# Two RMS norms inside a two-layer decoder trunk: the first weight block behind each multiplies the unnormalised x, and the division by the rms follows when the product is read out of PSUM

## What is computed

```python
def rms_norm(x, g):
    y = x * lax.rsqrt(jnp.mean(x * x, axis=-1, keepdims=True) + NORM_EPS)
    return y * g

def even_layer(h, ...):
    proj = rms_norm(h, norm_mix) @ w_in
    ...                                    # S5 state space model and block attention
    h = h + concatenate([y_a, y_b]) @ w_out
    return h + swiglu(rms_norm(h, norm_ffn), w_gate, w_up, w_down)      # norm 1, FFN of 2816

def odd_layer(h, ...):
    proj = rms_norm(h, norm_mix) @ w_in                                 # norm 2, 2756 columns
    ...                                    # RWKV-7 time mixing and sparse attention
    h = h + concatenate([y_c, y_d]) @ w_out
    return h + moe_swiglu(rms_norm(h, norm_ffn), router, e_gate, e_up, e_down)   # 8 experts, top 2
```

## Time and profile before

| | us |
|---|---|
| median of 3 runs | 1647.14 |
| lowest and highest of them | 1647.04, 1648.26 |
| the profiled execution, device time | 1645.62 |
| its span in the trace | 1643.8 |
| PE busy | 1550.2 (94% of the span) |
| DVE busy | 439.0 (27%) |
| ACT busy | 294.0 (18%) |

### The profile page before, as it was taken

How to read it: one execution, slowest core, us unless ns; L and a number is a source line. 1 busy time by engine, 2 the same in 40 slices (tenths; PEclk the granted TensorE clock), 3 DMA queues, 4 the chain that set the end, 5 groups by cost and what they waited for, 6 DMA issues and landing times.

```text
span 1643.8 us, 47174 instructions
## 1 busy us (share of the span) xinstructions
PE 1550.2 (94%) x22217; PEld 1464.2 (89%) x22217; DVE 439.0 (27%) x857; ACT 294.0 (18%) x515; POOL 19.3 (1%) x21
## 2 busy tenths in 40 slices
PE   7898999999946899999999999999999999999997
PEld 6667999998934788899999999999999999999996
DVE  6843354546387632100100100100100000100102
ACT  3233344334234211100000100100001001001002
POOL 0000000000001210000000000000000000000000
PEclk9999999999966998899999999999999999999998
DMA  9121555363300035599999999999999999999980
GB/s 316 58 99 53 205 204 181 128 230 105 147 0 1 3 111 212 189 385 356 377 373 359 374 383 348 372 382 357 369 380 360 369 384 355 363 384 357 370 318 28
DMA packets 135648, 425.22 MB, mean 259 GB/s; under 512 B 9786, under 2 KB 12964, under 8 KB 135332
## 3 DMA queue, kind: packets, MB, share of 16 engines
q1 hardware_dynamic: 133536, 420.59, 68.1%
q10 hardware_dynamic: 1924, 1.64, 0.4%
HBM read 421.18 MB, written 1.05 MB: 257 GB/s over the span
## 4 chain that ended last, share of the span: by engine, by line
PE 87%; DVE 9%; ACT 2%; issue 1%; DMA 0%; ACTq 0%; SPq 0%; DVEq 0%
PE bank L2242 34%; PE bank L2240 20%; PE bank L1885 5%; PE bank L1887 5%; PE bank L1886 5%; PE bank L2220 2%; PE bank L1860 2%; PE bank L2261 1%; PE bank L1629 1%; PE bank L1873 1%; PE bank L1795 1%; PE bank L1878 1%; PE bank L2228 1%; PE bank L1619 1%; DVE xnT L966 1%
## 5 line engine op out<-in xcount | busy, mean ns | idle before, releaser
L2242 PE MATMUL bank<-ring,yT 128*32 128x128 f32 x8064 | 889.1, 273 | 0.0
L2240 PE MATMUL bank<-ring,yT 128*32 128x384 f32 x8064 | 877.7, 487 | 1.0 <-ACT yT L886 1.0
L2242 PEld LDWEIGHTS bank<-ring,yT 128*32 128x32 f32 x8064 | 876.5, 110 | 0.0
L2240 PEld LDWEIGHTS bank<-ring,yT 128*32 128x32 f32 x8064 | 299.8, 109 | 11.7 <-issue 10.5
L1560 DVE TENSOR_TENSOR arena<-arena,bank 128x384 f32<-128x384 f32 x56 | 28.9, 551 | 635.2 <-PE bank L2242 635.2
L1887 PE MATMUL bank<-arena_r,ring_r 128*128 128x256 f32 x688 | 193.4, 281 | 0.0
L1885 PE MATMUL bank<-yT_r,ring_r 128*128 128x256 f32 x512 | 144.8, 283 | 5.2 <-DVE arena_r L1199 5.2
L1886 PE MATMUL bank<-yT_r,ring_r 128*128 128x256 f32 x512 | 144.5, 282 | 0.0
L1887 PEld LDWEIGHTS bank<-arena_r,ring_r 128*128 128x128 f32 x688 | 131.0, 190 | 0.0
L1194 DVE TENSOR_TENSOR ring_r<-ring,ring_r 128x2048 fp32r<-128x2048 f32 (+1 forms) x46 | 99.0, 2153 | 114.5 <-ACT ring_r L706 114.4
L902 ACT ACTIVATE yT<-bank 128x384 f32<-128x384 f32 x56 | 25.0, 491 | 560.5 <-PE bank L2261 560.5
(11 more groups left out here) (435 smaller groups left out, 1278.9 us busy)
## 6 DMA issues: line engine op xcount, KB each, us to landing
ring<-in_moe_w_gate SPq DMA_DIRECT2D x56, 2048.0 KB, 9.4
ring<-in_moe_w_up SPq DMA_DIRECT2D x56, 2048.0 KB, 9.4
ring<-in_moe_w_down SPq DMA_DIRECT2D x56, 2048.0 KB, 9.8
ring<-in_ffn_w_gate SPq DMA_DIRECT2D x5, 2048.0 KB, 7.8
ring<-in_ffn_w_up SPq DMA_DIRECT2D x5, 2048.0 KB, 7.8
ring<-in_ffn_w_down SPq DMA_DIRECT2D x5, 2048.0 KB, 8.9
ring<-in_o_w_in SPq DMA_DIRECT2D x5, 2048.0 KB, 7.8
ring<-in_e_w_in SPq DMA_DIRECT2D x4, 2048.0 KB, 16.8
```

Source lines behind the costliest of these rows:

```text
L2240: pe_.matmul(b[QUAD[m], 0:FM], x(m), w[:, 0:FM], start=start, stop=stop, skip_group_check=True)
L2242: last = pe_.matmul(b[QUAD[3], P * m:P * m + P], x(m), w[:, FM:FB], start=start and m == 0, stop=stop, skip_group_check=True)
```

## The change

At norm 1 and norm 2 the first block (gate 0, block 25) no longer waits for the rms. ACT writes `hT * g` rounded into the high part (`scaled_hi`, a copy with a scale per partition, eight instructions of 128 x 256), DVE writes `hT * g` minus that into the low part (`scaled_lo`, eight instructions of 128 x 256), both between the adds into `hT`. PE multiplies the first block with these. The products for the square sums stand inside its first half: four behind strip 1, two behind strip 2, two behind strip 3. The square root, the reciprocal and `xnT` come as before, and `split_xn` writes the normed high and low parts over the unnormalised ones, each half once PE has multiplied it; the second block (up 0, block 26) is the first to use them. The first block's result is multiplied by `rstd` by DVE (`by_rstd`, two instructions of 128 x 512): at norm 1 from PSUM into `gate_s`, where ACT then takes silu in place; at norm 2 from PSUM into `raw`, in place of `odd_copy(0)` and `odd_copy(1)` on ACT. The `keep_warm` products of both norms are gone, in front and behind. At norm 1 the high part lies in `arena`, not in `yT`, and the square sums have banks of their own (6 and 3).

```diff
-WARM = {"norm_in": [0, 5, 5, 5], "norm_out": [8, 12, 14, 10], "tilde": 3, "group_norm": 8,
+WARM = {"norm_in": [0, 5, 5, 5], "norm_out": [8, 0, 0, 10], "tilde": 3, "group_norm": 8,
...
+        def scaled_hi(m, gname, i):
+            act.wait_ge(sem("h_added"), 4 * m - 4 + i + 1)
+            for k in (2 * i, 2 * i + 1):
+                last = act_.activation(XHI[m][:, k, :], hT[:, k, :], ACT.Copy, scale=col(gname, k))
+            last.then_inc(sem("xhi_done"), 1)
+
+        def raw_norm(m, gname):
             for i in range(2):
+                scaled_hi(m, gname, i)
+            for i in range(4):
+                if i >= 2:
+                    scaled_hi(m, gname, i)
+                act_.activation(flat(xnT[:, 2 * i:2 * i + 2, :]), flat(hT[:, 2 * i:2 * i + 2, :]),
+                                ACT.Square).then_inc(sem("sq_done"), 1)
+            act.wait_ge(sem("ss_done"), m + 1)
+            act_.activation(rstd[:, :], ss_bank(m), ACT.Sqrt, scale=1.0 / D, bias=C("eps")).then_inc(
+                sem("rms_done"), 1)
+
+        def split_xn(m, i):
+            act.wait_ge(sem("xn_done"), 2 * m + i + 1)
+            act.wait_ge(sem("pair_used"), FIRST_HALF[m] + i + 1)
+            act_.activation(flat(XHI[m][:, 4 * i:4 * i + 4, :]), flat(xnT[:, 4 * i:4 * i + 4, :]), ACT.Copy).then_inc(
+                sem("xhi_done"), 1)
...
-        norm(1, lambda i: act.wait_ge(sem("h_added"), i + 1))
-        split_xn(1)
+        raw_norm(1, "e_norm_ffn")
+        split_xn(1, 0)
...
+                if c == 0:
+                    act.wait_ge(sem("gate_scaled"), 1)
                 for i in range(w // 2):
-                    last = act_.activation(gate_s[:, 512 * i:512 * i + 512], bank[i][:, :], ACT.Silu)
+                    s_ = gate_s[:, 512 * i:512 * i + 512]
+                    last = act_.activation(s_, bank[i][:, :] if c else s_, ACT.Silu)
...
             if h < 2 * len(ffn_steps) + 2:
                 split_hi(NFFN + h // 2, h % 2)
+            if h == 3:
+                split_xn(1, 1)
...
-        norm(2, lambda i: act.wait_ge(sem("h_added"), 5 + i))
+        raw_norm(2, "o_norm_mix")
...
-        split_xn(2)
+        split_xn(2, 0)
...
+            if m == 0:
+                split_xn(2, 1)
+            else:
+                odd_copy(2 * m)
+                odd_copy(2 * m + 1)
...
+        def scaled_lo(m, gname, i):
+            dve.wait_ge(sem("xhi_done"), 6 * m - 6 + i + 1)
+            for k in (2 * i, 2 * i + 1):
+                last = v.scalar_tensor_tensor(xlo[:, k, :], hT[:, k, :], col(gname, k), XHI[m][:, k, :].bitcast(f32),
+                                              MUL, SUB)
+            last.then_inc(sem("xlo_done"), 1)
...
+        def by_rstd(dst, b):
+            return v.tensor_tensor(dst, b[:, :].rearrange("p (k t) -> p k t", k=2),
+                                   rstd[:, None, :].to_broadcast([P, 2, T]), MUL)
...
         for i in range(4):
             add_h(i, bank[2 + i], i + 1)
+            if i:
+                scaled_lo(1, "e_norm_ffn", i - 1)
+        scaled_lo(1, "e_norm_ffn", 3)
         norm(1, "e_norm_ffn")
-        split_xn(1)
+        split_xn(1, 0)
...
+            if h == 3:
+                split_xn(1, 1)
+                dve.wait_ge(sem("pair_used"), 2)
+                for i in range(2):
+                    last = by_rstd(gate_s[:, 512 * i:512 * i + 512].rearrange("p (k t) -> p k t", k=2), bank[i])
+                last.then_inc(sem("gate_scaled"), 1)
...
+            if m == 0:
+                split_xn(2, 1)
+                for i in range(2):
+                    dve.wait_ge(*odd_ready(i))
+                    by_rstd(raw[:, i, :, 1:T + 1], bank[i]).then_inc(sem("odd_copied"), 1)
             shift(2 * m)
...
+        def square_sums(n, i):
+            pe.wait_ge(sem("sq_done"), 4 * n + i + 1)
+            for k in (2 * i, 2 * i + 1):
+                last = pe_.matmul(ss_bank(n), C("ones"), xnT[:, k, :], start=(k == 0), stop=(k == KD - 1),
+                                  skip_group_check=True)
+            if i == 3:
+                last.then_inc(sem("ss_done"), 1)
...
-        norm(1)
...
+                    if x == 0 and i and between:
+                        for z in {1: (0, 1), 2: (2,), 3: (3,)}[i]:
+                            between(z)
...
-                split_projection(n, bank[0:2], lambda x: pe.wait_ge(sem("xlo_done"), x + 1))
+                split_projection(n, bank[0:2], lambda x: pe.wait_ge(sem("xlo_done"), 6 if c else 2 * x + 2),
+                                 between=None if c else lambda z: square_sums(1, z))
...
-                split_projection(n, bank[2:4], lambda x: None)
+                split_projection(n, bank[2:4], lambda x: pe.wait_ge(sem("xlo_done"), 5 + x))
...
-        norm(2)
...
-            split_projection(NRAW - 5 + m, b, lambda x: pe.wait_ge(sem("xlo_done"), 2 + x + 1), sem("odd_proj"))
+            split_projection(NRAW - 5 + m, b, lambda x: pe.wait_ge(sem("xlo_done"), 6 + (5 + x if m else 2 * x + 2)),
+                             sem("odd_proj"), None if m else lambda z: square_sums(2, z))
```

More of the change, by code:

```diff
@@ L250, in trunk @@
     XLO = 14 * T + 8 * T + 2 * T + NT * HD + NT * 4
-    xhi = yT_r[:, :].rearrange("p (k t) -> p k t", k=KD)
+    XHI = {1: arena_r[:, 0:KD * T].rearrange("p (k t) -> p k t", k=KD), 2: yT_r[:, :].rearrange("p (k t) -> p k t", k=KD)}
     xlo = arena_r[:, XLO:XLO + KD * T].rearrange("p (k t) -> p k t", k=KD)
@@ L272, in ss_bank @@
     def ss_bank(n):
-        return bank[1 if n else 5][:, 0:T]
+        return bank[{0: 5, 1: 6, 2: 3, 3: 1}[n]][:, 0:T]
+    FIRST_HALF = {1: 0, 2: 2 * (NRAW - 5 - NFFN)}
     H_ODD = NH0 - 10
@@ L706, in split_hi @@
             act_.activation(pair(h, src.shape[1])[0], src, ACT.Copy).then_inc(sem("hi_done"), 1)
-        def split_xn(m):
-            for i in range(2):
-                act.wait_ge(sem("xn_done"), 2 * m + i + 1)
-                act_.activation(flat(xhi[:, 4 * i:4 * i + 4, :]), flat(xnT[:, 4 * i:4 * i + 4, :]), ACT.Copy).then_inc(
-                    sem("xhi_done"), 1)
+        def scaled_hi(m, gname, i):
[4 more added lines that the diff above has]
+        def raw_norm(m, gname):
+            for i in range(2):
+                scaled_hi(m, gname, i)
[12 more added lines that the diff above has]
+                sem("xhi_done"), 1)
         act.wait_ge(sem("proj_done"), 6)
@@ L754, in odd_copy @@
             if i < 7:
[L755 to L758, removed]
+                act.wait_ge(sem("shifted"), i - 1)
                 ins = act_.activation(raw[:, i % 2, :, 1:T + 1], b[:, :].rearrange("p (k t) -> p k t", k=2), ACT.Copy)
@@ L769, in _ @@
                 split_hi(NFFN + (H_ODD + 2 * m + 3) // 2, (H_ODD + 2 * m + 3) % 2)
-            odd_copy(2 * m)
-            odd_copy(2 * m + 1)
+            if m == 0:
[3 more added lines that the diff above has]
+                odd_copy(2 * m + 1)
             if m < 3:
@@ L1194, in split_lo, with split_xn @@
             v.tensor_tensor(lo, src, hi.bitcast(f32), SUB).then_inc(sem("lo_done"), 1)
[L1196 to L1200, removed]
+        def scaled_lo(m, gname, i):
[4 more added lines that the diff above has]
+            last.then_inc(sem("xlo_done"), 1)
+        def split_xn(m, i):
+            dve.wait_ge(sem("xhi_done"), 6 * m - 2 + i + 1)
+            v.tensor_tensor(flat(xlo[:, 4 * i:4 * i + 4, :]), flat(xnT[:, 4 * i:4 * i + 4, :]),
+                            flat(XHI[m][:, 4 * i:4 * i + 4, :]).bitcast(f32), SUB).then_inc(sem("xlo_done"), 1)
+        def by_rstd(dst, b):
+            return v.tensor_tensor(dst, b[:, :].rearrange("p (k t) -> p k t", k=2),
+                                   rstd[:, None, :].to_broadcast([P, 2, T]), MUL)
         for h in range(3):
@@ L1228, in _ @@
                 split_lo(NFFN + h // 2, h % 2)
+            if h == 3:
[4 more added lines that the diff above has]
+                last.then_inc(sem("gate_scaled"), 1)
         for i in range(4):
             add_h(i, bank[4 + i], 5 + i)
+            if i:
+                scaled_lo(2, "o_norm_mix", i - 1)
+        scaled_lo(2, "o_norm_mix", 3)
         norm(2, "o_norm_mix")
         split_lo(NRAW - 4, 0)
-        split_xn(2)
+        split_xn(2, 0)
         v.memset(raw[:, :, :, 0:1].rearrange("p b k o -> p (b k o)"), 0.0).then_inc(sem("raw_zero"), 1)
@@ L1887, in product3, with split_projection @@
             return pe_.matmul(dst, w[0], x[1], start=False, stop=stop, skip_group_check=True)
-        def split_projection(n, b, x_ready, first_bank_done=None):
+        def split_projection(n, b, x_ready, first_bank_done=None, between=None):
             w = view(n).shape[2] // P
+            xhi = XHI[1 if n < NRAW - 5 else 2]
             for x in range(2):
```

## The result

| | before | changed |
|---|---|---|
| median, us | 1647.01 (6 runs, 1645.70 to 1648.26) | 1635.16 (6 runs, 1633.96 to 1637.20) |
| ratio, 95% interval | | 0.993 (0.9920 to 0.9941) |
| profiled execution, us | 1645.62 | 1637.20 |
| its span | 1643.8 | 1635.4 |

The changed kernel is faster by 0.7%, some 11.5 us by the ratio (9.7 to 13.2). The forecast was 1638.6, 8.5 us less, with a range of 1634.5 to 1642.5. The two profiled executions stand 8.4 us apart, the medians 11.9: that difference is itself something to explain.

A forecast was written before the change was run, and what follows sets the result against it. PE was taken to set the pace, waiting around the two norms. Norm 1's 7.7 us plus norm 2's 0.8 (4.6 less clock costs 2.3 and 1.5) made 8.5: 1647.1 - 8.5 = 1638.6, range 1634.5 to 1642.5.

The forecast's parts named there:

- Norm 1, 7.7 us: At norm 1 the second FFN block (up 0) starts at 186.03 instead of 193.77, gaining 7.7 us.
- The order at norm 1: Rival: new waits spoil ACT's and DVE's order; with 2 us lost, gain 6.5, 1640.6; chance 0.12.
- The 0.3 us priced for this case: Silu's table loaded only after ACT's waits at norm 1: half 4 at 197.7, PE loses 0.3 us.
- Norm 2, 4.6 us before the clock: Block 26 ends at 404.86, 4.6 us earlier at full clock; after clock costs 0.8, between -0.6 and 3.1.
- the chain from the square root to block 26: At norm 2, ACT's and DVE's old order from square root to block 26 kept, taking 9.47 us.
- The sum for the first gap: Ahead of block 25, DVE's adds and low parts last until 374.75; PE idles from 369.21, 5.5 us.
- The clock, 2.3 and 1.5: Half clock behind norm 2's gaps costs 2.3 us (bounds 1.5 and 2.6) and 1.5 us (0 and 2.6).
- RWKV, attention and experts move up as a whole: Stages behind norm 2 start earlier; no gain or loss of their own was forecast.
- a stage after 640 us with another time: Sign of being wrong: a stage after 640 us takes another time than before.
- the silu table behind the scaling: Sign of being wrong at norm 1: silu's table load comes behind the scaling, not while ACT waits.
- the last one, from the profiled execution to the median: Last step of the sum: the median stands 1.5 us above the profiled execution, 1637.1, giving 1638.6.
- the clock up behind both gaps: Rival at norm 2: neither gap lowers the clock, gain 12.3, 1634.8; clock up in one or both 0.20.

The follow-up runs named there:

- norm1_only: The changed kernel with norm 2, its splits, read-outs and warm-up products put back as before; 1638.18 us, 0.9956 of before.
- warm_gaps: The changed kernel with 12 constant products ahead of block 25 and 7 ahead of block 26; 1632.59 us, 0.9924 of before.
- split38_early: The changed kernel with weight half 38 split while ACT and DVE wait for norm 2's square sums; 1632.81 us, 0.9922 of before.
- late37: The changed kernel with weight half 37 split behind x's low parts at norm 2, not ahead of the adds; 1632.52 us, 0.9918 of before.
- before_nowarm: The kernel before without the warm-up products in front of and behind the square sums of norms 1 and 2; 1647.86 us, ratio 1.0010.
- before_front0: The kernel before without the five constant products in front of norm 1's square sums; 1643.12 us, 0.9981 of before.
- norm2_only: The changed kernel with norm 1 put back as before; 1643.11 us, 0.9984 of before.
- warm_early2: The changed kernel with 12 constant products ahead of block 25, 2 ahead of block 26, half 38 split early; 1630.46 us, 0.9897 of before.
- changed_again: The changed kernel run once more, unedited, for a second trace; 1634.53 us, 0.9932 of before.

## Why the prediction was right, point by point

- **Norm 1, 7.7 us: right, by the mechanism told.** No pause behind the output products, sums inside the first half, 6.83 us from the square root to the second block, a gap of 1.25 (forecast 1.1) with the clock full. The second block starts 187.98 - 171.66 = 16.32 us behind the first product; forecast 186.03 - 169.76 = 16.27. norm1_only gave 7.2 by the ratio (5.1 to 9.2).
- **The order at norm 1: one rival came true, and cost 0.1 to 0.2 us.** I took the silu table to be loaded while ACT waits. It is loaded behind the waits. ACT's timeline in the changed kernel:

```profile
192.75 1.28 ACT L753 ACT_TABLE_LOAD   x1 [3.79 <-DVE arena L1239]
194.05 1.15 ACT L753 ACTIVATE arena<-arena 128x512 f32<-128x512 f32 x2
195.10 3.70 ACT L708 ACTIVATE ring_r<-ring 128x2048 fp32r<-128x2048 f32 x2
```

  DVE therefore had weight half 4 at 199.33, and the third block started at 199.57, 11.59 us behind the second, where 11.36 was forecast. This trace has no idle time of PE there, but nothing was to spare: in norm1_only, warm_gaps, split38_early and late37, the same code, the first product of the third block comes 0.24 us behind the one before it and not 0.12, and the block 11.45 us behind the second. The 0.3 us priced for this case were near. The load took 1.28 us and the next instruction began 0.02 later, as in the earlier trace rows; the trace shows no drain. With the one that the Trainium skill adds (ScalarE: Activation LUTs, What ACT_TABLE_LOAD costs) half 4 would have been ready some 1.1 us behind the third block's start, an estimate by the page's figure; PE did not wait so long in any trace.
- **Norm 2, 4.6 us before the clock: right in kind, 0.7 too small.** The first trace has 9.1 - 7.7 = 1.4 us for norm 2 with both falls of the clock in it, which cost 2.4 and 1.5, so 5.3 before the clock. The first gap is 5.54 (forecast 5.5), the second 3.41 (forecast 3.8). The term that was off is the chain from the square root to block 26: taken from the earlier trace rows as 9.47, it was 380.42 to 389.47, 9.05. That is no gain of the change. In the trace before, the last of ACT's five DMA issues took 1.34 us, so `split_hi` of half 38 came later than DVE was free for it; in all other traces it took 0.45, and norm1_only, before_nowarm and before_front0, with norm 2's chain as before, have 9.03 to 9.04. The sum for the first gap was right by luck: 370.75 and the terms named give 374.58, not 374.75, and what is missing, the 0.14 us between DVE's low part and PE's product, is in no term.
- **The clock, 2.3 and 1.5: right for the first trace (2.4 and 1.5), too large by 0.8 for the second (1.5 and 1.5).** Behind the gap of 5.5 us five traces have 1.5 to 2.4; the 2.3 taken from the nearest row, the gap of 5.69, is near their upper end. So norm 2 in all, forecast at 0.8, gave 1.4 and 2.3 us of the stretch in the two traces of the changed kernel and 2.6 (1.3 to 4.1) by the ratio of norm2_only: inside the bounds of -0.6 to 3.1, and the term that was furthest off in proportion. Both falls came; late37 and warm_gaps, each in its way, removed one or both and got the price back.
- **"RWKV, attention and experts move up as a whole": nearly.** The start of the router's products and of the experts' first ones, by line, in the changed kernel (L2255, L2309), then in the kernel before (L2186, L2240); the columns are shortest, median and longest in ns, then first and last start:

```profile
L2255 PE MATMUL bank<-arena,xnT x32: 255/256/323, 636.6 to 640.1; 128*128 128x8 f32 x32
...
L2309 PE MATMUL bank<-ring,yT x8064: 485/486/511, 661.8 to 1619.8; 128*32 128x384 f32 x197
```

```profile
L2186 PE MATMUL bank<-arena,xnT x32: 256/256/277, 644.2 to 647.7; 128*128 128x8 f32 x32
...
L2240 PE MATMUL bank<-ring,yT x8064: 486/486/510, 671.1 to 1629.1; 128*32 128x384 f32 x197
```

  From router to experts: 25.1 us now, 26.9 before. The experts: 958.0 both times. From their last product to the end of the span: 15.6 now, 14.7 before. Between, RWKV and attention were 0.4 us shorter in the first trace and 1.4 in the second. The prediction had named a stage after 640 us with another time, and the silu table behind the scaling, as signs of being wrong: both came, at the prices told here.
- **The median: 1638.6 forecast, 1635.16 and 1634.53 measured.** The step that was mis-sized is the last one, from the profiled execution to the median. Set against each other, the first trace of the changed kernel and that of before differ by: 1.9 lost ahead of norm 1, 9.1 gained in the stretch, 0.4 and 1.8 gained behind it, 0.9 lost at the end, in sum 8.4 (unrounded), which is the 8.5 of the forecast only because 1.9 lost and 1.3 gained outside the norms nearly balance. With the second trace: 1.6 lost, 10.0, 1.4 and 1.8 gained, 0.9 lost, in sum 10.6 (unrounded). That the first profiled execution came within 0.1 us of its forecast (1637.1) was luck. The kernel before happens to have a trace that reaches norm 1 early: twelve of the thirteen other traces reach it 1.2 to 2.3 us later, one 0.6, in code that is the same in all. Added to the 10.6, the 1.6 of that makes an estimate of some 12 us for a pair without this luck, and the medians differ by 11.9. The 1.5 us between profiled execution and median in the kernel before would then be that trace's early start, which is argued from these numbers and not tested. By the time alone another rival would have been believed: the clock up behind both gaps, a gain of 12.3 and 1634.8. The traces exclude it, for the clock fell behind both.

What stays open is why the stages behind differ. The router stretch took 26.9 in the traces of before, norm1_only and before_nowarm, 26.8 in that of before_front0, which all have norm 2 as before, and 25.1 in nine of the ten with norm 2 changed, but 26.9 in warm_early2. The half clock of that stage lasts 20.5 us in the five long ones and 17.1 in the nine short. One of ten traces with norm 2 changed is long, and all four with norm 2 as before: that looks like a link, but no edit touches the work of that stage, and no run here tests how the link would come about.

## What to carry to other kernels

A factor that is the same for a whole row of the result can be taken out of a product's input and put on its output, so that the product starts before the factor is known; but what this wins is the time of the work that then lies beside the factor's own chain. Put the work that feeds the chain (here the sums) as early into the covering block as its inputs allow, and nothing else on the queues that the chain runs over: the moved sums were worth 14.6 us, and each of two weight splits in the wrong place of DVE's list some 4 to 5 us of the stretch, 1.7 and 2.0 of the median. When a warm-up product is placed in front of work whose first inputs are ready, it is on the path (norm 1, 2.1 us); where that work has to wait anyway, it is free (norm 2).

## What the runs showed of the hardware

- At the two norms the granted clock fell from 1.00 to 0.50 behind waits of 2.85 (before_nowarm), 3.03, 3.41, 3.61 and 5.54 us and stayed at 1.00 behind 1.25, 1.69 and 2.73. Behind 3.41 us of waiting it was full for the first 1.5 us of work and only then fell, behind 3.40 us in changed_again for 0.4 us. Filling the waits with constant products, up to the last 0.4 us, kept it full.
- The same wait of 5.53 us cost between 1.5 and 2.4 us in five traces. Differences of one or two us between two traces of such a kernel need more than one trace of each: unchanged code ahead of norm 1 alone differed by up to 2.3 us.
- The issue of one DMA on ACT's queue took 1.34 us in the trace of the kernel before and 0.45 in the thirteen others for the same transfer (the broadcast of a row of 512).
